# First expert mixture of a fused two-block kernel: 896-column units, token rows to and from seven experts by way of device memory, larger weight packets

## What is computed

```python
def moe_swiglu(h, router_w, wg, wu, wd):
    t = h.reshape(-1, dm)                                  # 256 x 1024
    logits = (t @ router_w).astype(jnp.float32)            # 8 experts
    top_val, top_idx = lax.top_k(logits, TOP_K)            # TOP_K = 2
    gates = jax.nn.softmax(top_val, axis=-1)
    combine = jnp.sum(jax.nn.one_hot(top_idx, N_EXPERTS) * gates[..., None], axis=1)
    for e in range(N_EXPERTS):
        he = jax.nn.silu(t @ wg[e]) * (t @ wu[e])          # 1024 -> 3584
        out = out + (combine[:, e:e + 1] * he) @ wd[e]     # 3584 -> 1024
```

## Time and profile before

| | |
|---|---|
| median of 3 runs | 2449.31 us |
| the profiled execution's own time | 2451.69 us |
| its span, first to last instruction | 2449.9 us |
| mean granted TensorE clock | 0.990 of 2.4 GHz |
| PE busy | 2376.6 us, 97% |
| VectorE (DVE) busy | 621.4 us, 25% |
| ScalarE (ACT) busy | 309.1 us, 13% |
| read from device memory | 674.09 MB, mean 276 GB/s over the span |
| first mixture: first L792 matmul starts | 444.69 us |
| first mixture: last L807 matmuls end | 1377.67 us |

### The profile page before, as it was taken

How to read it: one execution, slowest core, us unless ns; L and a number is a source line. 1 busy time by engine, 2 the same in 40 slices (tenths; PEclk the granted TensorE clock), 3 DMA queues, 4 the chain that set the end, 5 groups by cost and what they waited for, 6 DMA issues and landing times.

```text
span 2449.9 us, 51613 instructions
## 1 busy us (share of the span) xinstructions
PE 2376.6 (97%) x24064; PEld 1531.1 (62%) x24064; DVE 621.4 (25%) x1135; ACT 309.1 (13%) x540; POOL 157.3 (6%) x173
## 2 busy tenths in 40 slices
PE   7999999999999999999999899989999999999998
PEld 5657777666666666666566687886668654444443
DVE  1530003201111101111010146661625232222223
ACT  1320001000000000000000133221424010000000
POOL 2000001000000000000000004340202000000000
PEclk9999999999999999999999999999999999999999
DMA  8684515699999999999999600021124469999995
GB/s 327 240 309 173 201 57 207 246 392 368 394 368 393 369 390 370 366 394 369 393 363 393 254 1 1 1 104 69 69 103 145 184 256 426 429 428 429 429 429 237
DMA packets 216966, 678.51 MB, mean 277 GB/s; under 512 B 5907, under 2 KB 9454, under 8 KB 204334
## 3 DMA queue, kind: packets, MB, share of 16 engines
q1 hardware_dynamic: 214320, 669.01, 70.8%
q0 software_dynamic: 2112, 6.05, 0.7%
q10 hardware_dynamic: 318, 0.10, 0.0%
HBM read 674.09 MB, written 1.05 MB: 276 GB/s over the span
## 4 chain that ended last, share of the span: by engine, by line
PE 84%; DMA 6%; DVE 5%; SPq 2%; ACT 2%; issue 1%; POOL 0%; DVEq 0%; POOLq 0%; ACTq 0%
PE ps L670 23%; PE ps L792 21%; PE ps L883 9%; PE ps L807 9%; DMA ring<-in_moe_wd 6%; PE ps L903 5%; PE ps L1097 3%; PE ps L870 3%; SPq L535 2%; PE ps L1251 1%; ACT arena L2314 1%; PE ps L1425 1%; PE ps L1430 1%; PE ps L1060 1%; PE ps L770 1%
## 5 line engine op out<-in xcount | busy, mean ns | idle before, releaser
L792 PE MATMUL ps<-ring,arena 128*32 128x256 f32 x10752 | 590.6, 379 | 0.5 <-DVE arena L1972 0.5
L792 PEld LDWEIGHTS ps<-ring,arena 128*32 128x32 f32 x10752 | 348.3, 110 | 232.8 <-issue 2.7
L670 PE MATMUL ps<-hT,ring 128*128 128x256 f32 (+1 forms) x1680 | 401.4, 399 | 5.8 <-issue 5.8
L670 PEld LDWEIGHTS ps<-hT,ring 128*128 128x128 f32 x1680 | 322.0, 192 | 87.5 <-issue 47.8
L2314 ACT ACTIVATE arena<-ps 128x512 f32<-128x512 f32 (+5 forms) x238 | 117.0, 523 | 1727.1 <-PE ps L792 781.6
L807 PE MATMUL ps<-ring,arena 128*32 128x256 f32 x5376 | 300.5, 379 | 2.3 <-DMA ring<-in_moe_wd 2.1
L807 PEld LDWEIGHTS ps<-ring,arena 128*32 128x32 f32 x5376 | 173.8, 110 | 118.2 <-DMA ring<-in_moe_wd 3.9
L1651 DVE TENSOR_TENSOR arena<-arena,ps 128x384 f32<-128x384 f32 x56 | 31.0, 554 | 592.2 <-ACT arena L2314 592.2
L883 PE MATMUL ps<-ring,arena 128*64 128x512 f32 x672 | 146.9, 592 | 0.0
L670 PE MATMUL ps<-arena 128*128 128x128 f32 (+1 forms) x1032 | 122.1, 276 | 7.4 <-ACT arena L2314 2.5
L2698 POOL TENSOR_SCALAR small<-small 128x1 f32<-128x1 f32 x18 | 5.8, 322 | 1901.6 <-ACT arena L2314 1901.4
(11 more groups left out here) (389 smaller groups left out, 2044.0 us busy)
## 6 DMA issues: line engine op xcount, KB each, us to landing
ring<-in_moe_wg SPq DMA_DIRECT2D x56, 2048.0 KB, 12.6
ring<-in_moe_wu SPq DMA_DIRECT2D x56, 2048.0 KB, 17.7
ring<-in_moe_wd SPq DMA_DIRECT2D x56, 2048.0 KB, 19.1
ring<-in_w_exp_up SPq DMA_DIRECT2D x22, 2048.0 KB, 18.0
ring<-in_w_exp_down SPq DMA_DIRECT2D x22, 2048.0 KB, 20.9
ring<-in_w_exp_gate SPq DMA_DIRECT2D x20, 2048.0 KB, 18.0
ring<-in_w_in SPq DMA_DIRECT2D x14, 2048.0 KB, 9.5
ring<-in_w_ada SPq DMA_DIRECT2D x12, 2048.0 KB, 16.2
```

The lines of the kernel that those rows point to most:

```text
L670: last = mm(outp, l, r, start=(i == 0), stop=(i == n - 1))
L792: last = mm(o_, x_[:, k, 32 * r:32 * r + 32], gu[:, :, k, :, q, :], start=(k == 0), stop=(k == KC - 1))
```

## The change

The first mixture gets programs of its own (`main_units`) on each engine; the old loop stays for further rounds alone.

- Units of `UW1` = 896 columns: 32 of them, n = 0 to 31, run on across the experts on PE: `up(0)`, then `up(n)`, `down(n-1)` for n = 1 to 31, then `down(31)`. `up` has 96 calls of 448 columns, `down` 84 of 256.
- The ring's six slots are now one unit: slots 0 and 1 gate and up for the first half of the input rows, 2 and 3 for the second half, 4 and 5 the down weights in parts of 4 and 3 rows. Each half has its own semaphore (`m1_uh`, `m1_up`, `m1_dh`, `m1_dn`). Gate and up pieces are 3584 bytes. For the down weights partition p takes rows 7p to 7p+6, so its pieces are 16 KB and 12 KB in a row; VectorE's multiply writes its result in the same order.
- Experts 1 to 7 get their inputs by device memory: GpSimd (POOL) copies `xn` into `xq`, and four indirect DMAs write the token rows (512 KB each) into `slot_inputs`, at places that VectorE works out (`slots_chosen`). For each expert SP reads 96 rows back in four loads of 96 KB, and VectorE transposes and scales them (`inputs_turned`). Expert 0 is gathered by matmul as before.
- Outputs of experts 0 to 6 go to `slot_rows` by four 96 KB stores each, issued by ScalarE; in the last expert POOL gathers them per token with four indirect DMAs of 512 KB, and VectorE adds them weighed by the gates (`rows_added`). Expert 7 is scattered by matmul as before.
- Ahead of all that, during the dense feed-forward layer, POOL fills `slot_inputs` with zeros (3.67 MB).

```diff
@@ SyncE @@
+            def main_units(first):
...
+                def fetch_up(n, h):
+                    e, j = divmod(n, U1)
+                    for t in range(2):
+                        s_ = 2 * h + t
+                        if n:
+                            sp.wait_ge(*at(("m1_uh", "m1_up")[h], n))
...
+                def expert_inputs(m):
+                    sp.wait_ge(*at("x_rows", 64))
+                    if m >= 3:
+                        sp.wait_ge(*at("xin_turned", m - 2))
+                    for q in range(4):
+                        sp.dma_start(xin[m % 2][32 * q:32 * q + 32, :].rearrange("p (r c) -> p r c", r=3),
+                                     slotx[m * C1:(m + 1) * C1, q * S:(q + 1) * S].rearrange("(r i) c -> i r c", r=3))\
+                            .then_inc(inc("xin_in"), 16)
...
+                for n in range(UNITS):
+                    if n + 1 < UNITS:
+                        for h in range(2):
+                            fetch_up(n + 1, h)
+                    if n % U1 == 1 and n // U1 + 1 < E1:
+                        expert_inputs(n // U1 + 1)
+                    if n:
+                        for h in range(2):
+                            fetch_down(n, h)
...
@@ TensorE @@
+            def main_units():
...
+                def up(n):
+                    e, j = divmod(n, U1)
...
+                    if j == 0:
+                        pe.wait_ge(*at("m1_xg", e + 1))
+                    if n:
+                        pe.wait_ge(*at("m1_act", n))
...
+                    for h in range(2):
+                        landed(2 * h, n)
+                        landed(2 * h + 1, n)
+                        gu = ring[:, 2 * h:2 * h + 2, 0:4 * UW1].rearrange("p m (k q n) -> p m k q n", k=4, q=4)
+                        for k in range(4):
+                            for r in range(3):
+                                for q in range(4):
+                                    o_ = ps[32 * q:32 * q + 32, r, 0:2 * QW].rearrange("p (m n) -> p m n", m=2)
+                                    last = mm(o_, x_[:, 4 * h + k, r, :], gu[:, :, k, q, :],
+                                              start=(h == 0 and k == 0), stop=(h == 1 and k == 3))
+                        last.then_inc(inc(("m1_uh", "m1_up")[h]), 1)
+
+                def down(n):
+                    e, j = divmod(n, U1)
+                    pe.wait_ge(*at("m1_aT", n + 1))
+                    if j == 0 and e:
+                        pe.wait_ge(*at("m1_y", e + 1))
...
@@ VectorE @@
+            def main_units(copy):
...
+                def inputs_turned(m):
+                    x_ = xgT[:, m % 2, 0:KC * C1]
+                    ve.wait_ge(*at("xin_in", 64 * m))
...
+                    V.transpose(x_, xin[m % 2]).then_inc(inc("xin_turned"), 1)
+                    ve.wait_ge(*at("xin_turned", m))
+                    x4 = x_.rearrange("p (r k i) -> p r k i", r=3, k=KC)
+                    V.tensor_tensor(x4, x4, gain[:, None, :, None].to_broadcast([P, 3, KC, 32]), ALU.mult).then_inc(inc("m1_xg"), 1)
+
+                def rows_added(c):
+                    ve.wait_ge(*at("y_rows", 32 * c + 32))
...
+                    if j == 2 and e + 1 < E1:
+                        inputs_turned(e + 1)
...
@@ ScalarE @@
+            def main_units():
...
+                def rows_kept(m):
+                    ac.wait_ge(*at("m1_dn", U1 * (m + 1)))
+                    if m:
+                        ac.wait_ge(*at("y_stored", 64 * m))
+                    act(ysb[:, 0:3 * S], flat[:, 3 * 512:3 * 512 + 3 * S], ACT.Copy).then_inc(inc("m1_y"), 1)
+                    if m < E1 - 1:
+                        ac.wait_ge(*at("m1_y", m + 2))
+                        for q in range(4):
+                            ac.dma_start(sloty[m * C1:(m + 1) * C1, q * S:(q + 1) * S].rearrange("(r s) n -> s r n", r=3),
+                                         ysb[32 * q:32 * q + 32, 0:3 * S].rearrange("p (r n) -> p r n", r=3)).then_inc(inc("y_stored"), 16)
...
@@ GpSimd @@
+            po.dma_start(slotx.rearrange("(p r) d -> p r d", p=P), ysb[:, None, :].to_broadcast([P, XROWS // P, D])).then_inc(inc("x_zeroed"), 16)
...
+            for i in range(4):
+                G.indirect_dma_start(slotx, bass.IndirectOffsetOnAxis(ap=idx_x[:, i:i + 1], axis=0), xq[:, i % NT, :], None)\
+                    .then_inc(inc("x_rows"), 16)
```

More of the change, by code:

```diff
@@ L32 @@
 UW = 512
+UW1, QW, ROWS1 = 896, 224, 7
 C1, C2 = 96, 64
@@ L557, in experts @@
-                def experts(p, end):
-                    for w in range(2 * U1):
-                        n = R * UNITS + 2 * U1 * p + w
-                        early = isinstance(p, int) and p == 0
-                        if w + 1 < 2 * U1:
-                            gate_up(2 * p + (w + 1) // U1, w + 1, None if early and w < 1 else n)
-                        elif not end:
-                            gate_up(2 * p + 2, 0, n)
-                        down(2 * p + w // U1, w, None if early and w < 2 else R * UNITS + 2 * U1 * p + w - 1)
@@ new lines, in expert @@
+                def expert(e, begin, end):
+                    for j in range(U1):
+                        n = R * UNITS + U1 * e + j
+                        if not (end and j == U1 - 1):
+                            for h in range(2):
+                                fetch_up(e + (j + 1) // U1, (j + 1) % U1, h, n + 1)
+                        if not (begin and j == 0):
+                            for h in range(2):
+                                fetch_down(e, j, h, n)
+                for h in range(2):
+                    fetch_up(0, 0, h, None)
@@ L1659, in expert @@
                     gathered(e + 1, 1 - b)
[L1661 to L1668 removed]
+                with ve.Fori(0, E1 // 2) as p:
+                    for b in range(2):
+                        expert(2 * p + b, b, R * UNITS + 2 * U1 * p + U1 * b)
```

329 lines of the change are left out of this document (247 added, 82 removed).

## The result

The changed kernel takes 2435.61 us (median of 5 runs, 2429.53 to 2438.31) against 2449.97 us for the kernel before, measured beside it (5 runs, 2447.60 to 2452.31). The ratio is 0.9935, with a 95% interval of 0.9923 to 0.9946: faster by 0.65%, or 14.4 us. The forecast was 2403 us with a range of 2388 to 2430. The sign was right; the gain was less than a third of the one forecast (46 us), and the time lies outside the range.

The account below looks back on a forecast made before the run. PE and DMA were both taken as full in the first mixture, PE losing 7.8 us an expert around gather and scatter. The terms summed to -46.3 us, giving 2405.4 us profiled and 2403 us median, range 2388 to 2430.

Parts of the forecast that it names:

- Term 1: Gathers and scatters leave PE in the first mixture, apart from the first gather and last scatter: -62.8 us.
- term 2: 448 columns in an `up` instruction on PE, so `up` takes 18.04 and `down` 9.07 us: -2.8 us.
- The rate of the new packets: Weight loads by DMA: 405 GB/s for 3584-byte pieces, 424 for 12 KB, 426 for 16 KB.
- Terms 3 and 4: Waits the gathers had covered, +1.9, +1.5 and +0.8 us; late loads at the stage's two ends, +3.3 and +2.0 us.
- Costed at nothing: Waits for token rows, VectorE and ScalarE work, zeros, and the time after the stage: no cost charged.
- term 5: Mid-stage, DMA needs 110.0 us an expert, 1.6 over PE; with the output gather and less the cushion, +9.8 us.
- the line: DMA time for one piece: 8.9 ns plus 37.0 ns per KB, from measured 2 KB and 16 KB pieces.
- The cushion of 6.5 us: The ring's lead in gate and up loads: 6.5 us of DMA lag cost nothing, once.
- from about the fifth: Sign in the profile after: PE waits for ring weights, none in the first experts, some from about the fifth on.
- PE-bound: First rival: PE holds the pace throughout, lag stays inside the cushion; -58.7 us, 2391 us; chance 0.30.
- The second rival: DMA becomes the bound, 3584-byte pieces moving at 387 GB/s, 113.4 us an expert; -20, 2429 us; chance 0.20.
- The third: Small transfers hold up the weights; slower from 1.2 us each, 2527 us at 2.6; chance 0.05 for 1.2 or more.

Follow-up runs that it names:

- experiment 11: Changed kernel with input loads for experts 1 and 2 alone and output stores for expert 0 alone; 2405.98 us, ratio 0.9815.
- experiment 1: Changed kernel with the four input loads kept for experts 1 and 2 alone, left out for experts 3 to 7; 2412.37 us, ratio 0.9838.
- experiment 2: Changed kernel with one 384 KB input load into 128 partitions for an expert, still 1 KB pieces, instead of four into 32; 2413.75 us, ratio 0.9845.
- experiment 4: Changed kernel with four 96 KB input loads for an expert, each over all 128 partitions instead of 32; 2416.18 us, ratio 0.9858.
- experiment 9: Changed kernel, whole computation, token rows written as quarters by 16 indirect writes, one 384 KB load over 128 partitions for an expert; 2415.42 us, ratio 0.9850.
- experiment 6: Changed kernel with output stores kept for expert 0 alone, 24 of 28 left out; 2426.29 us, ratio 0.9899.
- Experiment 5: Changed kernel, whole computation, with the same narrow input loads issued from ScalarE's queue instead of SP's; 2419.27 us, ratio 0.9868.
- experiment 3: Changed kernel with four 96 KB input loads over 32 partitions each, in 3 KB instead of 1 KB pieces; 2432.09 us, ratio 0.9925.
- Experiment 12: Kernel before with gathers, transposes and scatters of experts 1 to 6 left out, old units and packets kept; 2464.87 us, ratio 1.0057.

## Why the prediction failed

**What held.** Term 1 and term 2: the gathers are gone, and a unit takes 18.04 + 9.06 us where 18.04 + 9.07 were costed. The rate of the new packets, on which I said the gain hangs, was right where it could be read (405 forecast, 401 to 407 in stretches of gate and up loads; experiment 11 bounds the weights of an expert at 108.7 us). Terms 3 and 4 were right in their sums. The first wait was put at 1.9 + 0.7 + 2.6 = 5.2 us and is 5.55, the last at 1.5 + 2.0 = 3.5 and is 3.80. In the first, though, the product is ready at 463.69 + 1.36 = 465.05, some 2.3 us behind the matmuls (462.80) and not 1.9, since VectorE's multiply of 672 columns (L1855) is that long; it lies under the wait for the weights, which is over at 468.35. "Costed at nothing" held too: PE waits for no VectorE or ScalarE work in mid-stage, and from the last `down` to the end of the span it is 2433.8 - 1364.5 = 1069.3 us, against 1072.2 before. Nothing was given back there.

**What failed: term 5, the middle.** The stage takes 1364.5 - 444.55 = 919.9 us, where 932.98 - 46.3 = 886.7 were forecast: 33.2 too many (of which 2.9 came back behind the stage, so the profiled run is 30.3 over its forecast of 2405.4). By parts:

- An expert was to take 1.6 us over PE's 108.4 and takes 5.24 (113.64). Seven times 3.64 is **25.5**. The larger piece is the price of the input loads, charged at 1.5 us for four of them and measured at 4.15 (experiment 1): seven times 2.65 is 18.6. I had both ends in the text, 0.9 by the bytes and 10.4 by the nearest landing, and chose the low one with a line of time against size of piece. That line was right for the pieces (experiment 2: 1.07 against 1.1) and didn't hold how many partitions a transfer reaches.
- The rest of those 25.5, 7 us, the runs don't part further. DMA needs 107.0 us for the weights of an expert by the line, and I counted its 1.4 us of slack against PE as there for the row transfers. But paces add up onto 108.4 and not onto 107.0 (108.69 alone, 109.49 with stores, 113.64 with both). Either slack that lies in later units doesn't help, since a group holds the stream up in one piece and PE waits within two units of it (598.95 to 618.41). Or the weights take more than the line says: if DMA is the bound in the three runs, the paces with stores alone, with loads alone and with both give 109.49 + 112.34 - 113.64 = 108.2 us (an estimate), and there was hardly any slack. The landings lie between: behind the first group the gate and up loads of three units took 16.1, 15.6 and 15.7 us (issued at 508.0, 535.1 and 562.2), which is 0.4 us regained where 0.7 was counted.
- The cushion of 6.5 us was there, and one group used it up. A half of gate and up is needed 18.1 us after it is asked for; it landed 11.2 us after its issue at 480.8, and the one issued at 508.0, behind the first group, took 16.1 (13.3 with the wide loads of experiment 4). No wait of PE follows that group. The waits begin with the second and not "from about the fifth" expert on, because DMA falls behind by 5.2 us an expert and not by 1.6; with wide loads the same cushion lasts until 745.56 (experiment 9). So the cushion took in 4.9 us and not 6.5, and the middle is 1.6 us dearer by it (an estimate).
- **5.6** are the clock: 2.8 us each behind the first wait and the last one. None of my terms held a price for what follows a wait. (The slower units at 752.87 and 1073.76 lie within the 25.5.) In other runs waits as long cost less, 1.6 us behind 5.67 us (experiment 1), so the 5.6 are this execution's.
- 0.35 and 0.3 us of longer waits at both ends leave 1.5 of the 33.2, which is about what the cushion fell short by. The gather of the outputs was charged 5.1 us, and the three waits behind it are 4.0.

A rule had been set against this. The Trainium skill (DMA: Bandwidth & Descriptors, section Bandwidth) had led to an estimate of 1.1 us for each 96 KB transfer, and a result of -5.7 us; the change brought -14.4, nearer to that than to mine. The narrow loads do cost 4.15 / 4 = 1.04 us each. But the table isn't the reason: the same 96 KB over all partitions cost 0.9 / 4 = 0.23 (experiment 4), and the narrow stores, from ScalarE's queue, 0.33 to 0.38 (experiment 6). What I should have weighed is another page of the Trainium skill, SBUF — State Buffer, section Door 1: The DMA port swizzle. It states that partitions 0 to 31 reach 8 of the 16 ports, each with about 27 GB/s, 218 GB/s in all. An estimate from that page of the Trainium skill is 98 KB / 218 GB/s = 0.45 us a transfer, 1.8 for a group. Experiment 5 is near it (2.1 us from ScalarE's queue); the 4.15 in the weights' own queue is twice that, and why stays open.

**The rivals.** PE-bound (2391, chance 0.30) was too optimistic even with few row transfers: experiment 11 took 2405.98. The clock is 3.2 us of the difference (`up(1)` 19.76 and the last `down` 10.96 us, for 18.25 and 9.28); 6.3 us are waits behind the two groups of loads and the gather that this run keeps. The second rival (0.20) named the place, DMA in every expert, and its 2429 is nearest to the time, but by a mechanism that isn't there. The third (0.05) was the right mechanism: small transfers hold up the weights, at 1.04 us for the loads and about 0.35 for the stores, a mean of 0.7, where the kernel comes out even at 1.2. I gave it one price for both directions and a chance only from the point at which it makes the kernel slower. Its formula gives -46.3 + 56 x (0.7 - 0.375) = -28 us at that mean; the 7 us that aren't parted above and the 5.6 of clock, which it leaves out as well, bring it to -15.5, and -14.4 was measured. The range should have reached up through it: my sentence "most of a landing is latency" was no reason to end it at 2430.

## What to carry to other kernels

Beside a stream that fills DMA, cost a small transfer first by how many partitions it reaches. Wide ones cost about their bytes here (0.9 and 1.07 us for 0.39 MB, which is 0.97 at 405 GB/s), narrow ones four times that. Make it wide, even if that takes more writes elsewhere, and if it must be narrow take it out of the stream's queue. Don't set its cost against a percent of slack that is only worked out: here the paces with and without it added up onto the pace of the bound engine. And before taking work out from between two stages, look which load comes in under it: taken alone, the gathers were worth less than nothing.

## What the runs showed of the hardware that was not expected

- A load of 96 KB from device memory costs a saturated stream 1.04 us when it goes into 32 partitions, and 0.23 us when it goes into 128 (experiments 1 and 4). Fewer, larger pieces in 32 partitions hardly help (0.9 us, experiment 3). The DMA share stays at 1.05 to 1.17 meanwhile: a full share doesn't mean a full rate.
- The queue counts: the same narrow loads cost half when another engine issues them (2.1 against 4.15 us a group), though all share the 16 DMA engines. Whether it is the queue itself or the place among the weight loads that changes with it isn't shown. The Trainium skill (DMA: Bandwidth & Descriptors, section Rules for kernel authors) states that spreading transfers over issuing engines doesn't help bandwidth; here it is worth 16 us of the kernel's time (2435.61 to 2419.27), and the measurement decides.
- Narrow stores from ScalarE's queue cost 0.33 to 0.38 us each, narrow loads from the same queue 2.1 / 4 = 0.53 (experiments 6 and 5).
- Waits of 5.55 and 3.80 us were each followed by some 6 us at a granted clock of 0.50 and 2.8 us lost. Behind waits of 3.09 us (752.87) and 2.05 us (1073.76) 1.7 us were lost each time, behind 2.40 and 1.92 us (618.41, 731.49) nothing. The length of the wait alone doesn't give the loss: the first wait of experiment 1 was 5.67 us and `up(1)` took 19.82 us, 1.6 lost; its last one was 3.80 us and `down(31)` took 10.96, 1.7 lost.
- Left open: what the larger packets are worth by themselves. Experiment 12 was to give it as the rest, but its own waits hide it. Also open is why the narrow loads cost double in the weights' queue.
